# First modulation weights loaded by columns, scale ahead of shift; blocks scaled as they leave PSUM; three first product tiles begun over blocks 0 to 3 while the second half of the shift is still being loaded

## The chip, the cores and the metric

The kernel runs on one NeuronCore of a Trainium2 chip. The metric is the device time of one execution in microseconds (us), as the median of three runs; smaller is better. The engines are TensorE (PE in the rows; PEld is its weight load), VectorE (DVE), ScalarE (ACT), GpSimd (POOL) and SyncE (SP). Each runs its own instructions in order, and they wait for one another by semaphores.

## What is computed

One forward pass of two transformer-like blocks over 512 tokens of width 1024. The first block begins with an adaptive norm, and the change lies there and in the first projection behind it:

```
c_act = silu(c)
mod = (c_act @ w_ada[i] + b_ada[i]).reshape(bsz, 6, D_MODEL)
shift1, scale1 = mod[:, 0], mod[:, 1]          # columns 0..1023 and 1024..2047 of w_ada
u = rms_norm(x, ln1[i]) * (1.0 + scale1) + shift1
proj = u @ w_in                                # then split: ..., z, xbc, dt
dt = softplus(dt + dt_bias)                    # feeds the state space scan, with conv(xbc)
...                                            # scan, projections, FFN; the whole second block
```

## The kernel before

Activations are held by features: a matrix of 1024 x 512 is 8 blocks k of 128 features (partitions) by 512 tokens. Each fp32 product is three products of float32r parts: high x high, high weights x low activations, low weights x high activations. A high part is a rounded copy (ACT, into `whi` or `ahi`), a low part is what is left (DVE, into `wlo` or `alo`). A unit of weights is 1 MB, 1024 x 256, in `raw[0]` or `raw[1]`; it gives two tiles m of 128 features in PSUM banks G, 24 matmuls of 512 columns each (L560 to L562).

At the start `x` (xin, 2 MB) and the shift and scale columns of `w_ada` (eight row blocks `araw`, 1 MB each, 8 KB a partition) are loaded through the DMA queue of ACT (q10). SP's queue (q1) takes 24 vectors, then the 32 columns of `w_in` that give dt (128 B pieces), waits until six of the eight blocks of `w_ada` have landed (`first_landed[5]`), and then loads the first unit of x columns and, unit by unit as buffers come free, all later weights.

DVE multiplies each block of `w_ada` by its part of silu(c) and adds it to `adacc` (L1994 to L1999). TensorE sums `adacc` over the partitions, one column of ones as moving data for each of 16 blocks (L689). DVE makes `coef` = (1 + scale) * ln1 from it (L2028). Meanwhile `x` is turned to features (L652), once for the residual (`xT`) and once after the token factors of the norm (`xs`), and ACT copies the turned `xs` out of PSUM (L1306). Only with `coef` and the shift does ACT make the high parts of the eight blocks (L1320) and DVE the values and low parts (L2035, L1922).

`first_tiles()` on TensorE then goes over the blocks j = 0 to 7: two matmuls of dt (L705, L706, L708) and three of x tile 0 (L711 to L713), each block as soon as its low part is there. x tile 1 follows (`fm_tile`), with `turn_dt` (L724) in its middle: it brings dt back to tokens. Behind it come two tiles of the B and C unit and two of the z unit. TensorE's `keep_clock` matmuls (L646) give no result that is used.

Behind the dt tile hangs a chain in program order: ACT copies it out (L1330) and then splits the B and C unit (L1223), since that unit's high part goes into the buffer that held the dt weights; DVE makes its low part (L1891), the token form of dt (L2057 to L2073), with ACT between (L1343 to L1347), the six convolution steps of the x tiles (L2085), and only then the low part of the z unit (L1891).

## Time and profile before

| | before |
|---|---|
| median of 3 runs | 2228.36 us (2225.49 to 2229.49) |
| the profiled execution's own time | 2229.08 us |
| its span, first to last instruction | 2227.3 us |
| mean granted TensorE clock | 0.992 of full speed |
| TensorE busy in the span | 2194.3 us, 99% |
| first product matmul | 40.12 us after the span's start |
| first matmul of the z unit | 70.41 us |

Times in rows are microseconds from the span's start. A mean of one instruction is in nanoseconds. The granted clock is 1.00 at 2.4 GHz and 0.50 at 1.2 GHz.

### The profile page before, as it was taken

To read this page: it belongs to the slowest core of one execution; us is meant where nothing else is said; L and a number is where in the kernel's file an instruction comes from. 1 tells how busy PE (TensorE), PEld (TensorE's weight loads), DVE (VectorE), ACT (ScalarE), POOL (GpSimd) and SP (SyncE) were. 2 spreads that over 40 slices of the span, in tenths; PEclk is the share of its full clock that TensorE was granted. 3 is DMA by queue.
4 is the path that set the end of the run, shared out by engine and by line. 5 is a ranking of instruction groups with operands and counts; after the bars stand their busy time and mean duration, and the time that the engine had idled before them with its cause. 6 is when DMAs were issued, how large, how long until landed. Compare 5 with 4: busy or idle time off the path is not lost.

```text
span 2227.3 us, 28694 instructions
## 1 busy us (share of the span) xinstructions
PE 2194.3 (99%) x10942; PEld 1833.7 (82%) x10942; DVE 1297.0 (58%) x1831; ACT 858.4 (39%) x1223; POOL 25.2 (1%) x24
## 2 busy tenths in 40 slices
PE   7999999999999999999999999999999999999998
PEld 5888888888888898888888888889878678888887
DVE  5677777767673475434475344354777756434344
ACT  5655555543222342322343222234455444222224
POOL 0000000000000000000000000000001000000000
PEclk8999999999999999999999999999999899999999
DMA  7423323324543334233223322223121002233321
GB/s 254 134 80 106 98 95 104 102 76 157 183 151 103 104 116 132 95 95 97 93 93 101 108 94 95 95 95 93 44 74 39 20 32 83 95 97 99 107 85 67
DMA packets 208141, 222.10 MB, mean 100 GB/s; under 512 B 9413, under 2 KB 200330, under 8 KB 205994
## 3 DMA queue, kind: packets, MB, share of 16 engines
q1 hardware_dynamic: 206362, 210.26, 29.2%
q10 hardware_dynamic: 1680, 10.49, 1.2%
q8 instruction: 66, 1.08, 0.2%
q14 instruction: 33, 0.27, 0.0%
HBM read 218.57 MB, written 2.16 MB: 99 GB/s over the span
## 4 chain that ended last, share of the span: by engine, by line
PE 93%; DVE 3%; DMA 2%; issue 1%; ACT 1%; ACTq 0%; DVEq 0%; SPq 0%
PE G L560 25%; PE G L562 25%; PE G L561 25%; PE G L611 2%; PE G L613 2%; PE G L612 2%; PE G L1065 1%; PE X L778 1%; PE X L1082 1%; DMA araw<-in_w_ada 1%; PE G L574 1%; PE G L576 1%; PE G L575 1%; PE X L1072 1%; PE X L1048 1%
## 5 line engine op out<-in xcount | busy, mean ns | idle before, releaser
L560 PE MATMUL G<-ahi,whi 128*128 128x512 f32 x1472 | 584.6, 397 | 0.0
L562 PE MATMUL G<-ahi,wlo 128*128 128x512 f32 x1472 | 574.5, 390 | 0.0
L561 PE MATMUL G<-alo,whi 128*128 128x512 f32 x1472 | 574.2, 390 | 0.0
L1891 DVE TENSOR_TENSOR wlo<-raw,whi 128x2048 fp32r<-128x2048 f32 (+3 forms) x172 | 386.9, 2249 | 240.8 <-ACT whi L1223 237.8
L1223 ACT ACTIVATE whi<-raw 128x2048 fp32r<-128x2048 f32 (+3 forms) x176 | 330.1, 1876 | 443.0 <-PE G L562 423.5
L560 PEld LDWEIGHTS G<-ahi,whi 128*128 128x128 f32 x1472 | 277.4, 188 | 58.1 <-issue 2.1
L562 PEld LDWEIGHTS G<-ahi,wlo 128*128 128x128 f32 x1472 | 277.0, 188 | 58.4
L561 PEld LDWEIGHTS G<-alo,whi 128*128 128x128 f32 x1472 | 277.3, 188 | 57.8 <-issue 1.9
L560 PE MATMUL G<-hhi,whi 128*128 128x512 f32 x784 | 305.9, 390 | 0.5 <-issue 0.5
L562 PE MATMUL G<-hhi,wlo 128*128 128x512 f32 x784 | 305.1, 389 | 0.0
L561 PE MATMUL G<-hlo,whi 128*128 128x512 f32 x784 | 305.1, 389 | 0.0
L560 PEld LDWEIGHTS G<-hhi,whi 128*128 128x128 f32 x784 | 147.2, 188 | 31.5 <-issue 1.2
L562 PEld LDWEIGHTS G<-hhi,wlo 128*128 128x128 f32 x784 | 147.2, 188 | 30.7
L561 PEld LDWEIGHTS G<-hlo,whi 128*128 128x128 f32 x784 | 147.2, 188 | 30.5 <-issue 0.2
L611 PE MATMUL G<-whi,ahi 128*128 128x256 f32 (+2 forms) x320 | 92.1, 288 | 0.6 <-DVE alo L2474 0.5
L612 PE MATMUL G<-whi,alo 128*128 128x256 f32 (+2 forms) x320 | 90.0, 281 | 0.0
L613 PE MATMUL G<-wlo,ahi 128*128 128x256 f32 (+2 forms) x320 | 89.9, 281 | 0.0
L2085 DVE SCALAR_TENSOR_TENSOR cv<-pre,v1T,cv 128x512 f32<-128x512 f32 x96 | 71.6, 749 | 27.1 <-ACT pre L1355 22.2
L2387 DVE SCALAR_TENSOR_TENSOR xT<-G,xT 128x512 f32<-128x512 f32 x44 | 30.3, 690 | 97.8 <-PE G L562 97.8
L1625 ACT ACTIVATE gs<-gs 128x512 f32<-128x512 f32 x44 | 27.8, 632 | 153.4 <-DVE gs L2542 153.4
L1258 ACT ACTIVATE hhi<-sq 128x512 fp32r<-128x512 f32 x54 | 34.2, 633 | 129.7 <-DVE sq L2551 90.2
L2387 DVE SCALAR_TENSOR_TENSOR xT<-G,modT,xT 128x512 f32<-128x512 f32 x36 | 27.0, 749 | 73.8 <-PE G L562 73.5
(428 smaller groups left out, 2865.8 us busy)
## 6 DMA issues: line engine op xcount, KB each, us to landing
raw<-in_w_in SPq DMA_DIRECT2D x43, 1024.0 KB, 5.1
raw<-in_w_up SPq DMA_DIRECT2D x38, 1024.0 KB, 5.3
raw<-in_w_down SPq DMA_DIRECT2D x32, 1024.0 KB, 5.1
raw<-in_w_gate SPq DMA_DIRECT2D x22, 1024.0 KB, 5.1
braw<-in_w_ada SPq DMA_DIRECT2D x12, 1024.0 KB, 5.2
raw<-in_w_in SPq DMA_DIRECT2D x20, 512.0 KB, 4.4
araw<-in_w_ada ACTq DMA_DIRECT2D x8, 1024.0 KB, 18.0
bc<-acum_dram SPq DMA_DIRECT2D x8, 1024.0 KB, 6.9
```

The lines of the kernel that those rows point to most:

```text
L560: pe.matmul(bank[:], wh[:, j, f], rh[:, j, :], start=(j == 0), stop=False)
L561: pe.matmul(bank[:], wh[:, j, f], rl[:, j, :], start=False, stop=False)
L562: last = pe.matmul(bank[:], wl[:, j, f], rh[:, j, :], start=False, stop=(j == k - 1))
L611: pe.matmul(dst, rh[:, j, tk], wh[:, j, 0:n], start=(j == 0), stop=False)
L612: pe.matmul(dst, rl[:, j, tk], wh[:, j, 0:n], start=False, stop=False)
L613: last = pe.matmul(dst, rh[:, j, tk], wl[:, j, 0:n], start=False, stop=(j == k - 1))
L1223: act.activation(whi[s][:, 0:n], raw[s][:, 0:n], ACT.Copy).then_inc(hi_split, 1)
L1258: act.activation(dst, src, ACT.Copy).then_inc(val_hi, 1)
L1625: act.activation(gs[:, m, :], gs[:, m, :], ACT.Silu).then_inc(sg_ready, 1)
L1891: tt(wlo[s][:, 0:n], raw[s][:, 0:n], r32(whi[s][:, 0:n]), ALU.subtract).then_inc(lo_split, 1)
L2085: ins = stt(cv[:, m, :], pre[:, m, j:j + T], v1T[:, j, bass.ds(blk, 1)], cv[:, m, :], ALU.mult, ALU.add)
L2387: signal(stt(dst, src, gain, dst, ALU.mult, ALU.add), x_ready, "x", g_free[2 * s + m])
```

## The change

The first columns of `w_ada` are loaded in another order and shape: scale first (four pieces of two blocks, 4 KB a row), then the first half of the shift's columns (2 KB a row), then the first unit of x columns (now on ACT's queue too), then the second half of the shift in three pieces. The dt columns move ahead of 21 of the 24 vectors on SP's queue, and SP waits for the last piece of the shift before it loads the next unit.

The scale's first two blocks are multiplied on TensorE alone, the others on DVE, and the sums over partitions now move 128 columns of ones. ACT scales blocks 0 to 3 by `coef` as it takes them out of PSUM and adds the shift in a second operation that makes the high part; then blocks 4 to 7. ACT does all four scalings by the token factors (DVE did two), and loads the table of the square root before `x` has landed. GpSimd takes over the low parts of the dt columns and of the first unit. DVE makes each low part in one operation, and between those of blocks 0 to 3 it adds up the second half of the shift.

`first_tiles()` goes over blocks 0 to 3 with dt and both x tiles (eight matmuls a block), then sums the second half of the shift, turns the vectors, and goes over blocks 4 to 7 with dt and x tile 0, then x tile 1. `turn_dt` is four transposes in place of eight small matmuls, and DVE adds the two halves in one more operation.

```diff
-ahi, alo, xin, *araw = phase(*split_a, ("xin", [P, TB, D]), *((f"araw{u}", [P, UNIT]) for u in range(8)),
-                             ("adacc", [P, UNIT]))
-adacc = araw.pop()
-xn = [araw[k // 4][:, k % 4 * T:(k % 4 + 1) * T] for k in range(KB)]
+ahi, alo, xin, ascale, ashift, adacc = phase(*split_a, ("xin", [P, TB, D]), ("ascale", [P, KB, D]),
+                                             ("ashift", [P, 2, KB, D // 2]), ("adacc", [P, UNIT]))
+xc = [ascale[:, k // 2, k % 2 * T:(k % 2 + 1) * T] for k in range(KB)]
...
-    vec(v2[0:8, :], rows(a["ln1"][0]))
-    vec(v2[8:16, :], rows(a["ln2"][0]))
-    vec(v2[16:64, :], rows(a["b_ada"][0]))
+    sp.dma_start(v2[0:8, :], rows(a["ln1"][0])).then_inc(early_landed, 16)
+    sp.dma_start(v2[8:16, :], rows(a["ln2"][0])).then_inc(early_landed, 16)
+    sp.dma_start(v2[16:64, :], rows(a["b_ada"][0])).then_inc(early_landed, 16)
+    load(w_in[:, :, C_DT:C_DT + HEADS], n=HEADS)
...
-    load(w_in[:, :, C_DT:C_DT + HEADS], n=HEADS)
-    sp.wait_ge(first_landed[5], 16)
-    scan_turn(0, True, False, False)
+    loaded_by_act()
+    sp.wait_ge(first_landed[8], 16)
+    scan_turn(0, True, False, False, True)
...
+    mod = take_x(3)
+    pe.wait_ge(gone, 1)
+    pe.wait_ge(c_ready, 1)
+    pe.wait_ge(first_landed[0], 16)
+    for f in range(KB):
+        for k in range(2):
+            last = pe.matmul(mod[:, f:f + P], ascale[:, k, f * P:(f + 1) * P],
+                             cact[:, k:k + 1].broadcast_to([P, P]), start=(k == 0), stop=(k == 1))
+    last.then_inc(direct_done, 1)
+    pe.wait_ge(early_landed, 16 * EARLY_VECS)
+    pe.transpose(take_x(1)[:, 0:64], v2[0:64, :], ident[0:64, 0:64]).then_inc(aux_done, 1)
+    for k in range(4, KB):
+        turn_features(k, xin).then_inc(tile_done, 1)
     pe.wait_ge(scaled, TB)
-    for k in range(KB):
+    for k in range(4):
         turn_features(k, xs).then_inc(xn_done, 1)
...
+    def sums_by_ones(at, columns, used):
+        t["ada"].add()
+        pe.wait_ge(ada_acc, t["ada"].now())
+        for j, f in enumerate(columns):
+            last = pe.matmul(mod[:, at + j:at + j + P], adacc[:, f * P:(f + 1) * P], ones[:],
+                             start=True, stop=True)
+            if j >= len(columns) - used:
+                last.then_inc(ada_used, 1)
...
+    sums_by_ones(KB, range(KB, KB + 4), 2)
+    sums_by_ones(KB + 4, range(KB + 4, 2 * KB), 2)
+    turn_features(4, xs, take_g(1)).then_inc(xn_done, 1)
+    for k in range(5, KB):
+        turn_features(k, xs, take_x(k - 5)).then_inc(xn_done, 1)
+    sums_by_ones(2 * KB, range(4), 2)
...
-    keep_clock(1, xT[:, 0, :])
-    for f in (*range(KB, 2 * KB), *range(KB)):
-        if f % KB == 0:
-            t["ada"].add()
-            pe.wait_ge(ada_acc, t["ada"].now())
-        last = pe.matmul(X[3][:, f:f + 1], adacc[:, f * P:(f + 1) * P], ones[:, 0:1], start=True, stop=True)
-        if f % KB >= 4:
-            last.then_inc(ada_used, 1)
...
+        banks, wh, wl = [take_g(2 * sx), take_g(2 * sx + 1)], unit(whi[sx]), unit(wlo[sx])
+        keep_clock(FILL_FIRST, banks[0])
...
+        def products(m, j):
+            f = slice(m * P, (m + 1) * P)
+            pe.matmul(banks[m][:], wh[:, j, f], ahi[:, j, :], start=(j == 0), stop=False)
+            pe.matmul(banks[m][:], wh[:, j, f], alo[:, j, :], start=False, stop=False)
+            last = pe.matmul(banks[m][:], wl[:, j, f], ahi[:, j, :], start=False, stop=(j == KB - 1))
+            if j == KB - 1:
+                last.then_inc(tile_done, 1)
+        for j in range(4):
+            if j % 2 == 0:
+                pe.wait_ge(first_low, j // 2 + 1)
+            pe.wait_ge(act_ready, t["op"].now(j + 1))
+            steps(j)
+            for m in range(2):
+                products(m, j)
+        sums_by_ones(2 * KB + 4, range(4, KB), 2)
+        turn_vectors()
+        pe.wait_ge(x_free[2], 1)
+        keep_clock(FILL_SECOND, X[2])
+        pe.wait_ge(lo_split, t["n"].now())
+        for j in range(4, KB):
+            pe.wait_ge(act_ready, t["op"].now(j + 1))
+            steps(j)
+            products(0, j)
+        for j in range(4, KB):
+            if j == 6:
+                turn_dt()
+            products(1, j)
         t["op"].add(KB)
...
-            for half in range(2):
-                last = pe.matmul(bank[:, c * HEADS:(c + 1) * HEADS], ss[0:2 * HEADS, c * P:(c + 1) * P],
-                                 ident[0:2 * HEADS, half * HEADS:(half + 1) * HEADS],
-                                 start=(half == 0), stop=(half == 1))
+            last = pe.transpose(bank[:, 2 * c * HEADS:2 * (c + 1) * HEADS], ss[0:2 * HEADS, c * P:(c + 1) * P],
+                                ident[0:2 * HEADS, 0:2 * HEADS])
         last.then_inc(aux_done, 1)
...
-    for u in range(8):
-        act.dma_start(araw[u][:], a["w_ada"][0][u * P:(u + 1) * P, 0:UNIT]).then_inc(first_landed[u], 16)
+    for u in range(4):
+        ks = slice(2 * u, 2 * u + 2)
+        act.dma_start(ascale[:, ks, :], w_ada[:, ks, D:2 * D]).then_inc(first_landed[u], 16)
+    for u in range(2):
+        ks = slice(4 * u, 4 * u + 4)
+        act.dma_start(ashift[:, 0, ks, :], w_ada[:, ks, 0:D // 2]).then_inc(first_landed[4 + u], 16)
+    act.dma_start(unit(raw[1]), w_in[:, :, C_X:C_X + GW]).then_inc(landed[1], 16)
+    for u, ks in enumerate((slice(0, 4), slice(4, 6), slice(6, 8))):
+        act.dma_start(ashift[:, 1, ks, :], w_ada[:, ks, D // 2:D]).then_inc(first_landed[6 + u], 16)
...
+    act.activation(warm[:], epsT[:], ACT.Sqrt)
...
-    for b in range(2):
+    for b in range(TB):
         act.activation(xs[:, b, :], xin[:, b, :], ACT.Identity, scale=s4[:, b:b + 1]).then_inc(scaled, 1)
...
-    act.wait_ge(xn_free, 1)
-    for k in range(KB):
-        act.wait_ge(xn_done, k + 1)
-        act.activation(xn[k], G[k % 4][:], ACT.Copy).then_inc(g_free[k % 4], 1)
...
+    def scaled_block(k, bank, free):
+        act.wait_ge(xn_done, k + 1)
+        act.activation(xc[k], bank[:], ACT.Identity, scale=coef[:, k:k + 1]).then_inc(free, 1)
+    def shifted(half):
+        act.wait_ge(shift_ready, half + 1)
+        for k in range(4 * half, 4 * half + 4):
+            act.activation(ahi[:, k, :], xc[k], ACT.Identity, bias=modT[:, 0, k:k + 1]).then_inc(val_hi, 1)
+    act.wait_ge(coef_ready, 1)
+    for k in range(4):
+        scaled_block(k, G[k], g_free[k])
...
-    act.wait_ge(coef_ready, 1)
-    for k in range(KB):
-        act.activation(ahi[:, k, :], xn[k], ACT.Identity, scale=coef[:, k:k + 1], bias=modT[:, 0, k:k + 1])\
-            .then_inc(val_hi, 1)
-    t["val"].add(OWN)
-    act.wait_ge(val_hi, KB)
-    for k in range(OWN, KB):
-        act.activation(xn[k], xn[k], ACT.Identity, scale=coef[:, k:k + 1], bias=modT[:, 0, k:k + 1])\
-            .then_inc(own_value, 1)
...
+    shifted(0)
+    scaled_block(4, G[1], g_free[1])
+    for k in range(5, KB):
+        scaled_block(k, X[k - 5], x_free[k - 5])
...
+    shifted(1)
...
+    pool.wait_ge(x_ready, KB)
+    pool.wait_ge(scaled, TB)
+    pool.memset(pacc[:], 0.0).then_inc(gone, 1)
+    pool.wait_ge(hi_split, 1)
+    both = unit(whi[0], KB, 2 * HEADS)
+    pool.tensor_tensor(both[:, :, HEADS:2 * HEADS], unit(raw[0], KB, HEADS), r32(both[:, :, 0:HEADS]),
+                       ALU.subtract).then_inc(lo_split, 1)
+    for c in range(4):
+        if c % 2 == 0:
+            pool.wait_ge(*((hi_split, 2) if c else (first_hi, 1)))
+        cut = slice(c * T, (c + 1) * T)
+        pool.tensor_tensor(wlo[1][:, cut], raw[1][:, cut], r32(whi[1][:, cut]), ALU.subtract)\
+            .then_inc(first_low if c < 3 else lo_split, 1)
     pool.wait_ge(vec_landed, 16 * VECS)
     pool.tensor_copy(v3[0:XB, :].rearrange("b (r d) -> b r d", r=2),
                      dskip[:].unsqueeze(2).broadcast_to([XB, 2, HEAD_DIM])).then_inc(dskip_ready, 1)
-    pool.wait_ge(x_ready, KB)
-    pool.wait_ge(scaled, TB)
-    pool.memset(pacc[:], 0.0).then_inc(gone, 1)
...
-        dve.wait_ge(factor_ready, 1)
-        for b in range(2, TB):
-            ts(xs[:, b, :], xin[:, b, :], s4[:, b:b + 1], None, ALU.mult).then_inc(scaled, 1)
...
+    def weighted(dst, src, k, first=False):
+        c = cact[:, k:k + 1]
+        return ts(dst, src, c, None, ALU.mult) if first else stt(dst, src, c, dst, ALU.mult, ALU.add)
+    scale_acc, shift_acc = adacc[:, D:2 * D], [adacc[:, h * T:(h + 1) * T] for h in range(2)]
     dve.wait_ge(c_ready, 1)
...
+    dve.wait_ge(first_landed[1], 16)
+    for k in (2, 3):
+        link(weighted(scale_acc, ascale[:, k, :], k, k == 2))
+    token_factors()
+    dve.wait_ge(first_landed[2], 16)
+    for k in (4, 5):
+        link(weighted(scale_acc, ascale[:, k, :], k))
+    dve.wait_ge(first_landed[3], 16)
+    link(weighted(scale_acc, ascale[:, 6, :], 6))
+    link(dve.tensor_copy(v2T[:, 0:64], X[1][:, 0:64]))
+    dve.sem_inc(x_free[1], 1)
+    dve.wait_ge(direct_done, 1)
+    link(tt(modT[:, 1, :], X[3][:, 0:KB], badaT[:, KB:2 * KB], ALU.add))
+    for h in range(2):
+        weighted(scale_acc[:, h * T:(h + 1) * T], ascale[:, 7, h * T:(h + 1) * T], 7).then_inc(ada_acc, 1)
+    dve.wait_ge(first_landed[4], 16)
+    for k in range(4):
+        link(weighted(shift_acc[0], ashift[:, 0, k, :], k, k == 0))
+    dve.wait_ge(ada_used, 4)
+    link(tt(modT[:, 1, :], modT[:, 1, :], X[3][:, KB:2 * KB], ALU.add))
+    stt(coef[:], modT[:, 1, :], 1.0, ln1T, ALU.add, ALU.mult).then_inc(coef_ready, 1)
+    dve.wait_ge(first_landed[5], 16)
+    for k in range(4, KB - 1):
+        link(weighted(shift_acc[0], ashift[:, 0, k, :], k))
+    weighted(shift_acc[0], ashift[:, 0, KB - 1, :], KB - 1).then_inc(ada_acc, 1)
+    dve.wait_ge(ada_used, 6)
+    tt(modT[:, 0, 0:4], X[3][:, 2 * KB:2 * KB + 4], badaT[:, 0:4], ALU.add).then_inc(shift_ready, 1)
+    dve.wait_ge(xn_done, KB)
+    for k in range(4):
+        low(alo[:, k, :], ahi[:, k, :], xc[k], modT[:, 0, k:k + 1])
+        if k != 1:
+            dve.wait_ge(first_landed[6 + max(k - 1, 0)], 16)
+        link(weighted(shift_acc[1], ashift[:, 1, 2 * k, :], 2 * k, k == 0))
+        ins = weighted(shift_acc[1], ashift[:, 1, 2 * k + 1, :], 2 * k + 1)
+        if k < 3:
+            link(ins)
+        else:
+            ins.then_inc(ada_acc, 1)
+    dve.wait_ge(ada_used, 8)
+    tt(modT[:, 0, 4:KB], X[3][:, 2 * KB + 4:3 * KB], badaT[:, 4:KB], ALU.add).then_inc(shift_ready, 1)
+    dve.wait_ge(shift_ready, 2)
+    dve.sem_inc(x_free[3], 1)
+    for k in range(4, KB):
+        low(alo[:, k, :], ahi[:, k, :], xc[k], modT[:, 0, k:k + 1])
+    t["ada"].add(8)
+    t["hi"].add(2)
+    aux()
+    dve.tensor_copy(v2T[:, 64:P], X[1][:, P + 64:2 * P])
...
-    def value(k):
-        if k >= 2:
-            dve.wait_ge(act_ready, t["op"].now())
-        signal(ts(sq[:, k % 2, :], xn[k], coef[:, k:k + 1], modT[:, 0, k:k + 1], ALU.mult, ALU.add),
-               val_ready, "val")
-    value(0)
...
-    tt(heads(TMP), X[0][:, 0:P].rearrange("p (c h) -> p c h", c=TB), over(0), ALU.add).then_inc(prep_v, 1)
+    both = X[0][:, 0:2 * P].rearrange("p (c w h) -> p c w h", c=TB, w=2)
+    link(tt(heads(TMP), both[:, :, 0, :], over(0), ALU.add))
+    tt(heads(TMP), both[:, :, 1, :], heads(TMP), ALU.add).then_inc(prep_v, 1)
```

In TensorE's rows the stretch from the turned `xs` to the first block of products looked like this before (L646 `keep_clock`, L668 to L670 the vectors, L689 the sums, L706 on the products of block 0):

```order
L652 MATMUL G<-ident,xs 128x128 x32
L646 MATMUL X<-xT,ones 128x512 x5
L668 MATMUL X<-ident,v 128x128
L669 MATMUL X<-ident,v 128x128
L670 MATMUL X<-ident,v 128x77
L646 MATMUL X<-xT,ones 128x512
L689 MATMUL X<-ones,adacc 128x1 x16
L646 MATMUL X<-xT,ones 128x512
L706 MATMUL G<-ahi,whi 64x512
L708 MATMUL G<-alo,whi 32x512
L711 MATMUL G<-ahi,whi 128x512
```

With the change the same stretch of the same engine is this, up to block 0's first products (L687 sums, L653 `keep_clock`, L735 on the products):

```order
L659 MATMUL G<-ident,xs 128x128 x16
L687 MATMUL X<-ones,adacc 128x128 x8
L659 MATMUL G<-ident,xs 128x128 x4
L659 MATMUL X<-ident,xs 128x128 x12
L687 MATMUL X<-ones,adacc 128x128 x4
L653 MATMUL G<-xT,ones 128x512 x2
L735 MATMUL G<-ahi,whi 64x512
L737 MATMUL G<-alo,whi 32x512
L744 MATMUL G<-ahi,whi 128x512
```

The sums have moved in among the transposes, four of the 16 are gone from here (they come after block 3), the vectors' transposes have gone behind block 3 as well, and two `keep_clock` matmuls stand directly ahead of the products.

On DVE the stretch of the low parts was this before, from the first unit's low part on (L2035 values, L1922 low parts):

```order
L2020 TENSOR_TENSOR wlo<-raw,whi 128x1024
L2022 TENSOR_TENSOR wlo<-raw,whi 128x1024
L2025 TENSOR_TENSOR modT<-X,v2T 128x16
L2028 SCALAR_TENSOR_TENSOR coef<-modT,v2T 128x8
L2035 TENSOR_SCALAR sq<-araw,coef,modT 128x512 x2
L1922 TENSOR_TENSOR alo<-sq,ahi 128x512
L2035 TENSOR_SCALAR sq<-araw,coef,modT 128x512
L1922 TENSOR_TENSOR alo<-sq,ahi 128x512
```

With the change it is this, from the rest of the shift's first half on (L2071 a weighted sum, L2005 a low part):

```order
L2098 SCALAR_TENSOR_TENSOR coef<-modT,v2T 128x8
L2071 SCALAR_TENSOR_TENSOR adacc<-ashift,cact,adacc 128x512 x4
L2104 TENSOR_TENSOR modT<-X,v2T 128x4
L2005 SCALAR_TENSOR_TENSOR alo<-ascale,modT,ahi 128x512
L2071 TENSOR_SCALAR adacc<-ashift,cact 128x512
L2071 SCALAR_TENSOR_TENSOR adacc<-ashift,cact,adacc 128x512
L2005 SCALAR_TENSOR_TENSOR alo<-ascale,modT,ahi 128x512
L2071 SCALAR_TENSOR_TENSOR adacc<-ashift,cact,adacc 128x512 x2
L2005 SCALAR_TENSOR_TENSOR alo<-ascale,modT,ahi 128x512
```

The low parts of the weights are gone from DVE here, and two weighted sums now stand between one low part and the next, four times.

## Rows read from the trace of the kernel before

**Rows 1.** The chain that ended last, 0 to 110 us: start, length, what.

```profile
24.93 9.51 DMA raw<-in_w_in
34.47 1.06 ACT whi L1316
...
40.12 0.66 PE G L706
...
41.20 0.43 PE G L711
```

**Rows 2.** Timeline, 0 to 45 us: start, length, engine, line, operation, tile, count.

```profile
11.92 1.29 DVE L1994 TENSOR_SCALAR adacc<-araw,cact 128x2048 f32<-128x2048 f32 x1 [11.92 <-DMA araw<-in_w_ada]
...
13.77 1.28 ACT L1286 ACT_TABLE_LOAD   x1
...
15.27 2.72 ACT L1292 ACTIVATE xT<-G 128x512 f32<-128x512 f32 x4
...
18.11 2.19 ACT L1300 ACTIVATE xs<-xin,s 128x1024 f32<-128x1024 f32 x2
...
20.96 5.57 PE L652 MATMUL G<-ident,xs 128*128 128x128 f32 x32 [2.22 <-ACTq L1294]
...
31.33 2.48 DVE L1999 SCALAR_TENSOR_TENSOR adacc<-araw,cact,adacc 128x1024 f32<-128x1024 f32 x2 [0.81 <-DMA araw<-in_w_ada]
31.76 0.42 ACT L1311 ACTIVATE whi<-raw 128x256 fp32r<-128x256 f32 x1 [4.49 <-DMA raw<-in_w_in]
```

**Rows 3.** DMA queues, 12 to 27 us: packets, MB, share of 16 engines.

```profile
q10 hardware_dynamic: 802, 5.84, 95.2%
q1 hardware_dynamic: 779, 0.17, 5.6%
```

**Rows 4.** Groups of instructions by form, 0 to 130 us.

```profile
L2085 DVE SCALAR_TENSOR_TENSOR cv<-pre,v1T,cv 128x512 f32<-128x512 f32 x24 | 17.8, 750 | 3.0 <-ACT pre L1355 2.4
L1320 ACT ACTIVATE ahi<-araw,modT,coef 128x512 fp32r<-128x512 f32 x8 | 5.8, 800 | 1.9 <-DVE coef L2028 1.9
L1306 ACT ACTIVATE araw<-G 128x512 f32<-128x512 f32 x8 | 4.2, 600 | 0.2 <-ACT xT L1292 0.2
L757 PE MATMUL X<-xf 128*128 128x128 f32 x8 | 1.1, 275 | 0.0
```

**Rows 5.** GpSimd's groups by form, whole span.

```profile
L1867 POOL TENSOR_TENSOR wlo<-raw,whi 128x512 fp32r<-128x512 f32 x16 | 20.4, 1302 | 1739.5 <-ACT whi L1223 1739.5
L1860 POOL MEMSET pacc<- 128x4096 f32 x1 | 3.5, 3502 | 0.0
```

**Rows 6.** Busy time in stretches; PE, PEld, DVE, ACT, POOL, then the granted clock.

```profile
19.00:21.00 2.00, 0.04 (x1) 0.07 (x2) 1.97 (x1) 1.88 (x4) 0.00 (x0) 1.00 1.02 411
21.00:27.00 6.00, 6.00 (x34) 5.39 (x35) 5.92 (x3) 5.57 (x11) 0.00 (x0) 0.72 1.00 400
...
40.00:52.00 12.00, 11.88 (x41) 8.12 (x42) 6.14 (x11) 6.89 (x10) 0.00 (x0) 0.76 0.20 70
```

**Rows 7.** Timeline behind the dt tile, 51 to 71 us.

```profile
51.44 0.59 ACT L1330 ACTIVATE ss<-G 64x512 f32<-64x512 f32 x1 [5.07 <-PE G L706]
...
54.23 2.29 DVE L1891 TENSOR_TENSOR wlo<-raw,whi 128x2048 fp32r<-128x2048 f32 x1 [7.12 <-ACT whi L1223]
56.85 0.29 DVE L2057 TENSOR_TENSOR dts<-X,dtw 128x128 f32<-128x128 f32 x1 [0.32 <-PE X L724]
59.40 0.23 DVE L2061 TENSOR_SCALAR dts<-dts 128x128 f32<-128x128 f32 x1 [2.26 <-ACT dtw L1345]
...
67.82 2.28 DVE L1891 TENSOR_TENSOR wlo<-raw,whi 128x2048 fp32r<-128x2048 f32 x1
...
70.41 0.39 PE L560 MATMUL G<-ahi,whi 128*128 128x512 f32 x1
```

**Rows 8.** The chain that ended last, from the dt tile on.

```profile
51.17 0.23 PE G L706
...
54.84 1.90 PE X L724 x16
```

More of the change, by code:

```diff
@@ L695, in first_tiles, with steps @@
[L695 removed]
+            def first_tiles(turn_dt):
                 s = next_unit()
                 bank, wd = take_g(2 * s), unit(whi[s], KB, 2 * HEADS)
[L699 to L703 removed]
+                sx = slot[0]
+                slot[0] ^= 1
+                t["n"].add()
+                banks, wh, wl = [take_g(2 * sx), take_g(2 * sx + 1)], unit(whi[sx]), unit(wlo[sx])
+                keep_clock(FILL_FIRST, banks[0])
+                def steps(j):
+                    high, low, dst = wd[:, j, :], wd[:, j, 0:HEADS], bank[0:HEADS, :]
```

119 lines of the change are left out of this document (35 added, 84 removed).

## Prediction

> **What bounds the kernel now.** I read the chain that ended last first: apart from a few microseconds it is TensorE's products, so only a stretch in which TensorE stands still or does something else can give time. The start is such a stretch. There the chain is one transfer after another: the blocks of `w_ada`, then the first unit of x columns, which lands at 24.93 + 9.51 = 34.4 us, then the splits, coef and values, and the first product at 40.12 us [rows 1]. From there the products run without a gap, at first 0.43 us apart at 1.2 GHz, later 0.23 us at 2.4 GHz [rows 1, 8]. The windows say how long: a mean granted clock of 0.76 over 40 to 52 us is (1 - 0.76) / 0.5 x 12 = 5.8 us at the half rate, a loss of 2.9 us against the full one [rows 6].
>
> The second thing to see stands behind the dt tile, whose last matmul starts at 51.17 and ends about 51.4. TensorE has 19.0 us of own work until it starts the z unit at 70.41: 27 products, `turn_dt` (1.90 us), the 48 of B and C. The low part of the z unit is ready at 67.82 + 2.28 = 70.10, by a chain that begins with the end of the dt tile: copy and split on ACT, low part on DVE at 54.23, dt at 56.85 and again at 59.40, convolutions, z's low part [rows 7, 8]. That chain takes 70.10 - 51.4 = 18.7 us, and TensorE comes only 0.3 us after it. Two clocks thus run from the dt tile, nearly equally long, and the change shortens only one of them.
>
> **The change part by part.**
>
> *Transfers.* Seven blocks of `w_ada` landed in 31.33 - 11.92 us, 2.77 us for 1 MB [rows 2]. In the new order the scale's four pieces land at 11.9, 14.7, 17.5 and 20.2, the shift's first half at 23.0 and 25.8, the x unit about 28.7, the rest of the shift by about 34.5. The shorter rows may cost: the x unit (1 KB rows) came 34.44 - 31.33 = 3.1 us behind `w_ada`, 0.35 us more than the 8 KB rows; over the 4 MB of shift at most 1.4 us. I keep 34.5 to 36. The dt columns are 1024 pieces, 64 for each of 16 DMA engines. In 12 to 27 us the two queues moved 802 and 779 packets [rows 3], that is one for one, whatever their size; so those 64 go out beside the 64 packets of 4 KB an engine that make up the scale, and land about 20 us.
>
> The Trainium skill has the same rule (DMA: Bandwidth & Descriptors, Queues, rings and completion order): an engine goes round the rows that have work, but by whole packets of some 9 to 17 descriptors. By that the dt columns would be through in a few turns and land before 12 us. The count of packets in the rows agrees on the turns; nothing later depends on which it is, as ACT only comes to them at 24.5 us.
>
> *ACT and the norm.* The copies of `x` began at 15.27, behind a table load of 1.28 us [rows 2]. Moved ahead of `x`, the load still delays the squares by about 0.6, so I take 0.7 us: copies until 17.3. ACT then does four scalings at 1.10 (two took 2.19) in place of two, until 21.8, and four copies (2.72) until 24.5. TensorE turns blocks 0 to 3 of `xs` as banks come free, until 25.1.
>
> *Scale.* DVE is through with its part about 23.6. TensorE's eight sums follow the transposes: four fp32 matmuls of this form are 8 records in 1.1 us [rows 4], so 2.2 us at 2.4 GHz, about 3.4 at 1.2 GHz. coef is ready at 27.7 or 29.0.
>
> *Shift, first half.* Behind coef DVE still has four weighted sums of 0.75 [rows 4], TensorE four sums, DVE the bias: 32.2 or 34.1. Beside that ACT has four scaled copies (0.6) and the unit's high part in two halves of 1.06 (2.1) [rows 1, 4]. Then 0.8 for the high part of block 0 and 0.8 for its low part: ready at 34.0 to 35.7; I take 34.8. GpSimd needs 1.30 for the piece of low weights that block 0 uses [rows 5], begun about 32, its memset of 3.5 us being over by 28.2: hidden. The two `keep_clock` matmuls ahead take 0.9 each or, at 1.2 GHz, 1.7; only then they reach past the low part, to about 37.
>
> *First half of the products.* Eight matmuls a block are 1.84 us at 0.23, but DVE needs low part and two weighted sums, 3 x 0.75 = 2.25 us, a block. DVE leads: low parts at 34.8, 36.8, 39.0, 41.3, last sum 42.8. This is later than the transfers land, even at 36. Sums 1.1, bias 0.3, ACT 0.7, low part 0.8, semaphores 0.2: block 4 is ready at 45.9. The vectors' transposes and one `keep_clock` lie in this gap. Three blocks of five matmuls (1.15 each) and two more give the end of the dt tile: 45.9 + 3.45 + 0.65 = 50.0 us, against 51.4. A lead of 5.2 us in the first low part has shrunk to 1.4, because blocks 4 to 7 wait for a second round of sum, bias, high and low part. Bounds: 49.2 with 2.4 GHz throughout, 52.1 if `keep_clock` and the first block run at 1.2 GHz.
>
> *Behind the dt tile.* TensorE now has only 15 products left of the x tiles (it did the other 12 before) and a shorter `turn_dt` (0.5): it would reach B and C at 50.0 + 4.0 = 54.0, but their low part needs 5.1 us from the dt tile (54.23 + 2.29 - 51.4), so 55.1. It ends them at 66.0, and z's low part is there at 50.0 + 18.7 = 68.7. The one DVE operation that is added lies where it waited for `turn_dt` (0.32) [rows 7]. z begins at 68.7 in place of 70.41: 1.7 us gained. The products that moved ahead of the dt tile have become waits of 1.1 and 2.7 us.
>
> *The clock.* Waits are not free here. Ahead of 20.96 TensorE waited 2.2 us [rows 2], and the next 6 us had a mean clock of 0.72, which is 3.4 us at 1.2 GHz [rows 6]. Behind z's wait the same would cost 3.4 x 0.5 = 1.7 us. Whether a wait of 2.7 us brings this each time, one execution does not say; I charge half, 0.85.
>
> *Sum.* 2229.08 - 1.7 + 0.85 = 2228.2 for an execution like the profiled one. This lies 0.7 above the median shown, so 2227.5. Everything behind z is the same code with the same waits. Its own range: the dt tile's 49.2 to 52.1 and the clock's 0 to 1.7 give -2.5 to +2.2 us, 2225.0 to 2229.9. Executions differ by about as much (2225.49 to 2229.49). A change under 0.2%, 4.5 us, is what a measurement of this kernel cannot tell from none.
>
> **The rivals.**
>
> *The lead is carried through (faster).* If the first product comes 6 us earlier and neither DVE nor the chain behind dt holds TensorE up, the time is 2228.4 - 6 = about 2222. For it: the transfers bound the start, and they no longer do. Against it: block 4 cannot be ready before a second round of sums, and 18.7 us behind the dt tile is in the rows. It needs a dt tile that ends by 46. Chance 0.15.
>
> *The clock stays at 1.2 GHz (slower).* TensorE waits for banks, for coef and for sums from 18 us on, and before, the clock was at 0.50 for the first 5.8 us of the products although `keep_clock` had run ahead of them [rows 1, 6]. If it stays low through blocks 0 to 3, these take 32 x 0.43 = 13.8 us in place of 9: from 37 to 50.8, block 4 at 53.9, the dt tile at 58, z at 76.7, 6 us late, 2234. It decides once the low stretch reaches past about 43 us. Against it: 32 transposes without a pause ended the low stretch at about 25 us while they ran [rows 2, 6]. Chance 0.07.
>
> The Trainium skill (TensorE: Matmul & The Clock Gate, HAM oscillation) warns of this: a kernel whose bursts are cut by waits is throttled again at each, so work cut in two halves pays twice. The row of 21 to 27 us agrees that a wait is paid for afterwards.
>
> *The dt columns land as late as before (slower).* They used to land about 31.8 us, where ACT splits them (L1311) [rows 2]; if a thousand small packets do so still, ACT stands in front of the scaled blocks until then, coef or not: high part at 32.2, scaled blocks to 34.7, unit to 36.8, block 0's low part at 38.3, 3.5 us later than taken, z 1.8 us later than before, 2231. Rows 3 speak against it. Chance 0.08.
>
> **How the numbers follow.** No measurable change has 0.70 from the first case. The predicted time is its 2227.5. The range reaches from 2222.8, into the faster case, to 2232, over the late dt columns, and leaves out the clock case and half of the faster one. Faster by over 0.2%: most of 0.15 and a tail of the first case, 0.17. Slower: 0.07, part of 0.08 and a tail, 0.12. Within: 0.71.
>
> **What would show it.** In the changed kernel's profile: dt columns split by ACT at 24.5, not later; coef at 27.7 to 29.0; first product at 34 to 37; 2.2 us from one low part to the next on DVE; a gap of TensorE ahead of block 4; the end of the dt tile at 49 to 52; waits ahead of the B and C unit and of z, with DVE's L1972 as releaser; a clock of 0.5 somewhere behind 69 us. The prediction is wrong if z starts before 66 or after 73 us, or if anything behind z has changed its length.

## The result, and the profile after

The changed kernel takes 2250.93 us (median of 5, 2249.21 to 2252.07) against 2228.36 before: a ratio of 1.0102, 95% interval [1.0091, 1.0114]. The median of before is one of 5 executions too, not of 3. The change makes the kernel 22.6 us slower, outside the predicted range. The profiled execution took 2252.07 us, span 2250.3.

The chain of work that ended last in the changed kernel, 0 to 60 us (start, length, what), names the cause in its first rows:

```profile
0.74 0.45 ACTq L1326
1.23 0.52 ACTq L1329
...
3.53 2.07 ACTq L1332
5.63 4.98 ACTq L1332
10.64 5.07 ACTq L1333
15.74 4.22 ACTq L1335
19.99 4.34 ACTq L1335
24.36 1.43 ACTq L1335
25.82 1.28 ACT L1337
27.12 0.19 ACT cact L1337
```

ACTq is ACT's own instruction stream while it hands a transfer to its queue. The rows up to 25.79 compute nothing: a single issuing instruction takes up to 5 us, and ACT does nothing else meanwhile. L1326 loads `x`, L1329 the scale, L1332 and L1335 the halves of the shift, L1333 the x unit. From 3.53 to 25.79 us ACT is held, and its Silu, the squares and all that hangs on them come that much later. The timeline of ACT in the changed kernel (start, length, engine, line, operation, tile, count):

```profile
28.80 1.04 ACT L1344 ACTIVATE sq<-xin 128x1024 f32<-128x1024 f32 x1
...
33.72 2.72 ACT L1351 ACTIVATE xT<-G 128x512 f32<-128x512 f32 x4
36.56 4.27 ACT L1359 ACTIVATE xs<-xin,s 128x1024 f32<-128x1024 f32 x4
```

The copies `xT` began at 15.27 before [rows 2]; they are 18.45 us late here. Coef is made on DVE at 47.19, and the first product starts on TensorE at 54.49 in place of 40.12 [rows 1]. DVE's and TensorE's timeline from there:

```profile
47.19 0.62 DVE L2098 SCALAR_TENSOR_TENSOR coef<-modT,v2T 128x8 f32<-128x8 f32 x1
...
53.19 1.15 DVE L2005 SCALAR_TENSOR_TENSOR alo<-ascale,modT,ahi 128x512 fp32r<-128x512 f32 x1 [0.94 <-ACT ahi L1380]
54.27 1.50 DVE L2071 TENSOR_SCALAR adacc<-ashift,cact 128x512 f32<-128x512 f32 x1
55.81 1.66 DVE L2071 SCALAR_TENSOR_TENSOR adacc<-ashift,cact,adacc 128x512 f32<-128x512 f32 x1
57.50 0.75 DVE L2005 SCALAR_TENSOR_TENSOR alo<-ascale,modT,ahi 128x512 fp32r<-128x512 f32 x1
...
66.77 2.74 DVE L2005 SCALAR_TENSOR_TENSOR alo<-ascale,modT,ahi 128x512 fp32r<-128x512 f32 x4 [0.87 <-ACT ahi L1380]
```

```profile
71.80 0.59 ACT L1401 ACTIVATE ss<-G 64x512 f32<-64x512 f32 x1 [3.23 <-PE G L735]
76.93 0.50 PE L567 MATMUL G<-ahi,whi 128*128 128x512 f32 x1 [1.14 <-DVE wlo L1972]
90.43 0.50 PE L567 MATMUL G<-ahi,whi 128*128 128x512 f32 x1 [2.32 <-DVE wlo L1972]
```

The copy of the dt tile starts at 71.80 (51.44 before [rows 7]), the B and C unit at 76.93, z at 90.43 (70.41 before [rows 7]): 20.0 us late. The span is 2250.3 - 2227.3 = 23.0 us longer. The other 3 us I put down to the clock in the attention part; the windows of before and of the changed kernel, in this order, with the granted clock third from the end of a row:

```profile
1680.00:1820.00 140.00, 134.69 (x772) 103.46 (x770) 100.53 (x294) 67.27 (x182) 20.37 (x16) 0.94 0.10 31
```

```profile
1680.00:1820.00 140.00, 132.94 (x781) 105.99 (x780) 103.84 (x314) 67.20 (x182) 20.38 (x16) 0.91 0.11 34
```

Against 2.4 GHz, 0.94 costs (1 - 0.94) x 140 = 8 us, 0.91 costs 13. The code there is the same, though the two windows lie 20 us apart in it. In the other versions below this stretch cost 5 to 10 us (0.93 to 0.96), whatever they did at the start, so I take it as the scatter of one execution and not as an effect of the change; no run shows this by itself.

**What holds ACT.** Before, the eight issues of `w_ada` took 4.34 us together, and the Silu came at 7.91:

```profile
1.23 4.34 ACTq L1277 DMA_DIRECT2D araw<-in_w_ada  x8
...
7.91 0.18 ACT L1279 ACTIVATE cact<-X 128x8 f32<-128x8 f32 x1 [1.03 <-PE X L640]
```

The page counts what each queue moved in the whole execution. ACT's is q10; first before, then after:

```profile
q10 hardware_dynamic: 1680, 10.49, 1.2%
```

```profile
q10 hardware_dynamic: 4784, 11.54, 1.4%
```

10% more bytes, but 4784 / 16 = 299 pieces for each of the 16 DMA engines in place of 105. A row that lies in one piece in memory is one piece of the transfer: 8 KB each in `w_ada`'s blocks before; 4 KB in the scale, 2 KB in the shift and 1 KB in the x unit now. The queue rows of the changed kernel up to the end of the last issue, 0 to 25.8 us:

```profile
q10 hardware_dynamic: 2771, 8.49, 87.4%
```

So (4784 - 2771) / 16 = 126 pieces for an engine were still waiting when ACT was let go. The same count at the end of the second shift issue (10.6 us) gives 120, of the x unit's (15.7) 153. Before, 1680 pieces less the 297 moved by 5.6 us leave 86, and no issue took over 0.6 us. My theory was now: **an issue ends only when the queue has room for its pieces, some 120 to 155 for each DMA engine.** The rival: the transfers in smaller rows, or the new order of the work, make the start late, and ACT's long rows only show it.

### The profile page after: what moved, and what is told of

It is laid out like the page before. It is cut to its first block, busy times and chain, and to the rows that moved or that the text cites. A ratio compares the mean times of both kernels' runs of the same rounds, so it can differ in the third digit from the quotient of the medians.

```text
span 2250.3 us, 28698 instructions
## 1 busy us (share of the span) xinstructions
PE 2192.2 (97%) x10951; PEld 1834.6 (82%) x10951; DVE 1295.5 (58%) x1840; ACT 858.8 (38%) x1223; POOL 31.4 (1%) x29
## 3 DMA queue, kind: packets, MB, share of 16 engines
q10 hardware_dynamic: 4784, 11.54, 1.4%
## 4 chain that ended last, share of the span: by engine, by line
PE 92%; DVE 4%; ACT 2%; ACTq 1%; issue 1%; DMA 0%; DVEq 0%; SPq 0%
PE G L567 25%; PE G L569 25%; PE G L568 24%; PE G L618 2%; PE G L619 2%; PE G L620 2%; PE G L1116 1%; PE X L829 1%; PE X L1133 1%; PE G L581 1%; PE G L583 1%; PE G L582 1%; PE X L1123 1%; PE X L1099 1%; PE X L837 0%
## 5 line engine op out<-in xcount | busy, mean ns | idle before, releaser
L2169 DVE SCALAR_TENSOR_TENSOR cv<-pre,v1T,cv 128x512 f32<-128x512 f32 x96 | 71.7, 749 | 27.2 <-ACT pre L1426 22.2
L2471 DVE SCALAR_TENSOR_TENSOR xT<-G,xT 128x512 f32<-128x512 f32 x44 | 30.4, 690 | 98.1 <-PE G L569 98.1
```

Of the source, the lines that this page charges most:

```text
L2169: ins = stt(cv[:, m, :], pre[:, m, j:j + T], v1T[:, j, bass.ds(blk, 1)], cv[:, m, :], ALU.mult, ALU.add)
L2471: signal(stt(dst, src, gain, dst, ALU.mult, ALU.add), x_ready, "x", g_free[2 * s + m])
```

## The experiments

Five of the eleven transfers go to SP's queue, in the same order; six with 33 + 4 x 17 + 33 = 134 pieces for each DMA engine stay with ACT. SP hands the five over once the scale's third piece has landed; nothing else changes.

```diff
# SP, behind the vectors
+sp.wait_ge(first_landed[2], 16)
+sp.dma_start(ashift[:, 0, 4:8, :], w_ada[:, 4:8, 0:D // 2]).then_inc(first_landed[5], 16)
+sp.dma_start(unit(raw[1]), w_in[:, :, C_X:C_X + GW]).then_inc(landed[1], 16)
+for u, ks in enumerate((slice(0, 4), slice(4, 6), slice(6, 8))):
+    sp.dma_start(ashift[:, 1, ks, :], w_ada[:, ks, D // 2:D]).then_inc(first_landed[6 + u], 16)
...
```

> The change with its last five early transfers (second piece of the shift's first half, x unit, three pieces of the shift's second half) issued by SP in the same order, once the scale's third piece has landed; ACT keeps x, four scale pieces and one shift piece. Theory 1 (ACT is held while it issues: its queue holds only about 130 outstanding pieces for each DMA engine, and the change gives it about 300): ACT is free at about 5.6 us in place of 25.8, c is there at 8 in place of 27.1, the first product comes at 35 to 38 in place of 54.5, and the time falls by about 20 us, to 2228 to 2232. Theory 2 (the transfers themselves, or the order of the work behind them, make the change late): c is early, but the first product stays behind 48 us and the time above 2243.

Measured: 2230.98 us against 2227.20 of before on the same chip, ratio 1.0016 [1.0007, 1.0025]. Of the 22.6 us above before, 3.8 are left: some 19 are gone. The timeline of this version:

```profile
3.50 2.28 ACTq L1335 DMA_DIRECT2D ashift<-in_w_ada  x1
5.81 1.28 ACT L1337 ACT_TABLE_LOAD   x1 [5.81 <-issue]
...
17.57 4.27 ACT L1359 ACTIVATE xs<-xin,s 128x1024 f32<-128x1024 f32 x4
21.74 2.72 ACT L1351 ACTIVATE xT<-G 128x512 f32<-128x512 f32 x4
24.58 0.42 ACT L1366 ACTIVATE whi<-raw 128x256 fp32r<-128x256 f32 x1
...
36.73 0.42 PE L740 MATMUL G<-ahi,whi 128*64 128x512 f32 x1 [0.32 <-DVE alo L2005]
```

The rival is out: with the same transfers in the same row sizes, and the same order of work, the first product is not late when ACT doesn't issue them. (SP's wait plays no part in this: the last run below leaves it out, in a later version, and nothing comes late.)

The dose between: the second shift piece stays with ACT (167 pieces), four transfers go to SP.

```diff
+act.dma_start(ashift[:, 0, 4:8, :], w_ada[:, 4:8, 0:D // 2]).then_inc(first_landed[5], 16)
```

> As the run before, but the second piece of the shift's first half stays with ACT: only x unit and the shift's second half go by SP. Theory 1: ACT's last issue ends about 10.6 us, 5 us later than in the other version, as the record of the changed kernel shows for that piece; c at 12, squares and copies of x 4 us later; time 0 to 4 us above the other version. Theory 2: no difference between the two.

Measured: 2235.61 us, ratio 1.0036 [1.0023, 1.0050]. That one transfer costs 4.6 us of the median, because its issue takes 5.2 in place of 0.4 on SP:

```profile
3.58 1.94 ACTq L1334 DMA_DIRECT2D ashift<-in_w_ada  x1
5.55 5.18 ACTq L1335 DMA_DIRECT2D ashift<-in_w_ada  x1
```

z starts at 75.80, 4.03 us later than the 71.77 of the version with five.

The other way round: the kernel before, with nothing changed but the size of the pieces. Padding in the SBUF cuts the same 1 MB transfers into rows of 2 KB.

```diff
-*((f"araw{u}", [P, UNIT]) for u in range(8))
+*((f"araw{u}", [P, 4, 512 + 8]) for u in range(8))
...
-act.dma_start(araw[u][:], a["w_ada"][0][u * P:(u + 1) * P, 0:UNIT])
+act.dma_start(araw[u][:, :, 0:512], a["w_ada"][0][u * P:(u + 1) * P, 0:UNIT].rearrange("p (c n) -> p c n", c=4))
...
```

> The kernel before with one thing changed: the eight blocks of w_ada are laid down in the SBUF with 32 bytes of padding behind every 512 numbers, so that the same eight transfers of 1 MB move in pieces of 2 KB in place of 8 KB, in the same order; nothing else differs. 33 pieces an engine for x and 33 for each block: 297 in place of 105. Theory 1: ACT is held until some 25 us, its Silu is at about 26 in place of 7.9, the sums of eight blocks on DVE end about 46 in place of 34, and the time rises by 12 to 16 us, to 2240 to 2245. Theory 2 (the count of pieces does not hold ACT): ACT ends its issues at about 5.6 us as before and the time stays within 3 us of 2228.

Measured: 2236.71 us, ratio 1.0047 [1.0032, 1.0062], where I had 2240 to 2245. The timeline and the queue row of the whole execution:

```profile
1.23 17.25 ACTq L1277 DMA_DIRECT2D araw<-in_w_ada  x8
18.50 1.28 ACT L1279 ACT_TABLE_LOAD   x1 [18.50 <-issue]
```

```profile
q10 hardware_dynamic: 4752, 10.49, 1.3%
```

The bytes and the number of transfers are those of before, the pieces 297 an engine, and the eight issues take 17.25 us in place of 4.3. ACT was free at 18.5, not at my 25: I had carried the changed kernel's end over, which has 1 MB more to move and smaller rows at its end. By 18.5 us q10 had moved 2287 pieces, so (4752 - 2287) / 16 = 154 were left. The first product came at 49.14, 9.0 us late, and the median rose by 9.5. DVE reads the padded rows in the times of before (the last two sums take 2.48 in both) and, once c is there, never waits for a transfer, so neither of these makes it late. This shows the count of pieces as the cause by itself, without any other part of the change.

The same in rows of 4 KB (169 pieces):

```diff
-*((f"araw{u}", [P, UNIT]) for u in range(8))
+*((f"araw{u}", [P, 2, 1024 + 8]) for u in range(8))
...
```

> The kernel before with its eight blocks of w_ada moved in pieces of 4 KB in place of 8 KB (32 bytes of padding behind every 1024 numbers), all else alike: 33 + 8 x 17 = 169 pieces for each DMA engine in ACT's queue. Theory 1 (a limit of about 130 outstanding pieces an engine): the last issues wait until about 40 of them have landed, which is when x has landed: ACT is free at 9 to 10 us in place of 5.6, far before the 18.5 of the version with 2 KB pieces, and Silu is at 11. The sums on DVE started at 11.9 anyway; the time rises by 0 to 4 us. Theory 2 (smaller pieces merely cost more issue time in proportion to their count, 17.25 us for 264): about 9 us for 136, ACT is free at 10 too, but the single issues would be of equal length, 1.1 us each, in place of short ones first and long ones last.

Measured: 2229.25 us, ratio 1.0009 [0.9999, 1.0018]. ACT's issues in this version, two windows of its timeline and its queue row from 0 to 11.3 us:

```profile
1.22 1.04 ACTq L1277 DMA_DIRECT2D araw<-in_w_ada  x2
```

```profile
5.51 2.51 ACTq L1277 DMA_DIRECT2D araw<-in_w_ada  x1
```

```profile
q10 hardware_dynamic: 827, 3.26, 77.0%
```

Half a microsecond each while there is room, then 2.5 to 3 us each, not 1.1 throughout: a piece has no fixed price, a full queue has. (2704 - 827) / 16 = 117 were waiting at the end. ACT was free at 11.3, somewhat later than my 9 to 10, and this hardly costs anything, since the sums of `w_ada` on DVE, which were the chain, began at 11.92 anyway [rows 2].

Then ACT's Silu alone, ahead of the last six transfers of the changed kernel.

```diff
+aux()
+act.activation(cact[:], X[0][:, 0:KB], ACT.Silu).then_inc(c_ready, 1)
 for u in range(2):
     ks = slice(4 * u, 4 * u + 4)
     act.dma_start(ashift[:, 0, ks, :], w_ada[:, ks, 0:D // 2]).then_inc(first_landed[4 + u], 16)
...
-aux()
-act.activation(cact[:], X[0][:, 0:KB], ACT.Silu).then_inc(c_ready, 1)
```

> The change with one instruction moved: ACT's Silu stands ahead of its last six transfers instead of behind all of them. The squares of x still stand behind the issues. Theory 1: c at about 8 us, the scale's weighted sums on DVE are done by 24 us; ACT still issues until about 26 us, the scaled x (xs) comes at 40 as in the change, and the first product at 45 to 48 in place of 54.5; time 2240 to 2245. Theory 2: as the change, 2250, or, if only c counted, 2230.

Measured: 2247.62 us, ratio 1.0089 [1.0074, 1.0105]; c at 7.79, but ACT's last issue still ends at 25.7 and the first product comes at 52.19. It missed the 45 to 48 and the 2240 to 2245. DVE makes two of the scale's sums and then stands 15.6 us in front of the reciprocal of the norm, which needs ACT's squares:

```profile
15.43 1.28 DVE L2071 SCALAR_TENSOR_TENSOR adacc<-ascale,cact,adacc 128x1024 f32<-128x1024 f32 x1
32.35 0.18 DVE L2048 RECIPROCAL s<-s 128x4 f32<-128x4 f32 x1 [15.64 <-ACT s L1345]
...
45.16 0.16 DVE L2097 TENSOR_TENSOR modT<-modT,X 128x8 f32<-128x8 f32 x1 [4.03 <-PE X L687]
```

But this isn't what sets the first product: DVE has all its sums of the scale by 38.4, goes on to the shift's, and then waits 4.03 us for TensorE's, which stand behind the turned `xs`. `xs` is made until 39.3 here and until 40.8 in the changed kernel, and from there it is 13 to 14 us to the first product in either (turning, sums, coef, the first half of the shift). My 45 to 48 left too little for these. An early c is worth 2 to 3 us while the squares stand behind the issues.

**What was left of the prediction's error.** The version with five by SP ends 3.8 us above before, where I had 0.9 below. Its DVE shows one place, its GpSimd the other side of it:

```profile
35.84 0.75 DVE L2005 SCALAR_TENSOR_TENSOR alo<-ascale,modT,ahi 128x512 fp32r<-128x512 f32 x1 [0.94 <-ACT ahi L1380]
36.51 1.52 DVE L2071 TENSOR_SCALAR adacc<-ashift,cact 128x512 f32<-128x512 f32 x1
38.06 0.75 DVE L2071 SCALAR_TENSOR_TENSOR adacc<-ashift,cact,adacc 128x512 f32<-128x512 f32 x1
```

```profile
34.76 1.27 POOL L1937 TENSOR_TENSOR wlo<-raw,whi 128x512 fp32r<-128x512 f32 x1
35.99 1.76 POOL L1937 TENSOR_TENSOR wlo<-raw,whi 128x512 fp32r<-128x512 f32 x1
```

GpSimd's last part starts during DVE's low part and takes 0.5 us longer than the one before; DVE's TENSOR_SCALAR, 0.49 elsewhere, ends at 38.03, 0.3 behind the end of that part at 37.75. In the changed kernel the three DVE rows shown above lose 1.15 - 0.75, 1.50 - 0.49 and 1.66 - 0.75, 2.3 us in all. The test gives DVE the low part, in two halves, in the time in which it waited for sums; GpSimd's four parts go:

```diff
+dve.wait_ge(first_hi, 1)
+tt(wlo[1][:, 0:half], raw[1][:, 0:half], r32(whi[1][:, 0:half]), ALU.subtract).then_inc(first_low, 1)
+dve.wait_ge(hi_split, 2)
+dve.wait_ge(lo_split, 1)
+tt(wlo[1][:, half:UNIT], raw[1][:, half:UNIT], r32(whi[1][:, half:UNIT]), ALU.subtract).then_inc(lo_split, 1)
 dve.wait_ge(ada_used, 6)
...
```

> The version with five transfers by SP, and the low part of the first x unit made by DVE in two halves of 1.15 us (while it waits for the shift's sums, 31.8 to 34.7 us) in place of four parts on GpSimd. Theory A (GpSimd's work on the SBUF holds DVE up, 1.5 us in place of 0.5 for the TENSOR_SCALAR behind the first low part): that one takes 0.5 again, the step from the first low part to the second is 2.2 us in place of 3.0, everything behind it 0.8 earlier, time 0.5 to 1 us less. Theory B (it was long for another reason, as its first use or the DMA's writing): the duration stays at 1.5 and the time unchanged or up.

Measured: 2229.45 us, ratio 1.0008 [0.9999, 1.0017].

```profile
36.50 0.75 DVE L1999 SCALAR_TENSOR_TENSOR alo<-ascale,modT,ahi 128x512 fp32r<-128x512 f32 x1 [0.94 <-ACT ahi L1380]
37.17 0.48 DVE L2065 TENSOR_SCALAR adacc<-ashift,cact 128x512 f32<-128x512 f32 x1
```

The operation takes 0.48 with the same operands and the same transfers running; the next low part follows after 1.97 us in place of 3.01. So GpSimd's work beside it was the reason. The gain does not go through, though: the first low part itself starts 0.66 us later, since DVE's second half of the weights' low part stands ahead of the bias, and z starts at 71.41, 0.36 us earlier and not 0.8. The intervals of the two versions overlap; the medians, 1.5 us apart, show a direction at most.

The Trainium skill (SBUF — State Buffer, Who interferes with whom) has such interference as a lock: GpSimd uses DVE's second pair of ports, and whoever comes first holds it for the whole instruction. The rows fit a lock: GpSimd's 1.27 and DVE's 0.49 both grow while the other is at work, and DVE's ends just behind GpSimd's. They don't prove one: DVE's low part at 35.84 begins 0.19 us before the end of GpSimd's third part (34.76 + 1.27) and takes its usual 0.75, and spans on GpSimd are rough.

Next, which of the two clocks behind the dt tile counts. For blocks 4 to 7, the dt tile's eight matmuls go first:

```diff
 for j in range(4, KB):
     pe.wait_ge(act_ready, t["op"].now(j + 1))
     steps(j)
+for j in range(4, KB):
     products(0, j)
```

> The version with five transfers by SP, and for blocks 4 to 7 the dt tile's eight matmuls run ahead of the x tiles' 24. Theory A (the chain of 18.7 us behind the dt tile sets the start of z, TensorE's own work does not): the dt tile ends at 51.4 in place of 53.6, no wait ahead of B and C, z starts at 70.0 to 70.3 in place of 71.8, time 1.5 to 2 us less. Theory B (TensorE's own work sets it): z starts at 71.8 as before.

Measured: 2227.07 us, ratio 0.9999 [0.9989, 1.0008]. In this execution block 4's low part starts at 47.25, 0.9 us earlier than in the version without the edit (48.12), because its bias came 2.3 us earlier, with the clock up (below). The dt copy is at 50.73, 3.5 us behind it in place of 5.0, and z at 69.36, 18.6 behind the copy: 1.5 us of the 2.4 are the edit's. The wait ahead of B and C is gone, that ahead of z is 1.70. The chain behind the dt tile sets z.

All together, and TensorE's sums at two places ahead of transposes that nobody waits for:

```diff
-for k in range(4):
+for k in range(2):
     turn_features(k, xs).then_inc(xn_done, 1)
 sums_by_ones(KB, range(KB, KB + 4), 2)
 sums_by_ones(KB + 4, range(KB + 4, 2 * KB), 2)
-turn_features(4, xs, take_g(1)).then_inc(xn_done, 1)
+for k in range(2, 4):
+    turn_features(k, xs).then_inc(xn_done, 1)
 for k in range(5, KB):
     turn_features(k, xs, take_x(k - 5)).then_inc(xn_done, 1)
+turn_features(4, xs, take_g(1)).then_inc(xn_done, 1)
 sums_by_ones(2 * KB, range(4), 2)
...
```

> Five transfers by SP, the low part of the first unit by DVE, dt tile first, and TensorE's order changed at two places: the scale's sums ahead of turning blocks 2 and 3 of the scaled x, and block 4 turned after blocks 5 to 7 so that the sums of the shift's first half do not wait for ACT's scaled block 1. Each should bring what it removes from the chain: coef at 27.2 (28.6), bias of the first half at 32.5 (34.7), first low part at 33.6 (35.8), dt tile's end at 48 (53.6), z at 67 (71.8); time 2226 to 2227, level with or 1 us under the kernel before. If TensorE's own work sets z, it comes at 69 and the time is 2228.

Measured: 2225.86 us against 2227.35, ratio 0.9990 [0.9981, 0.9999]: the one version whose interval lies under 1, if barely. Coef is at 27.28 and z at 68.25 (I had 67). What each of the two orders of TensorE is worth was not run by itself, and coef moves with the clock too: 28.61 and 27.66 in two versions with the same code up to there. The bias of the first half came at 33.81, not 32.5, which the next run looks at: the second half of DVE's low part stood ahead of it.

```diff
-dve.wait_ge(hi_split, 2)
-dve.wait_ge(lo_split, 1)
-tt(wlo[1][:, half:UNIT], raw[1][:, half:UNIT], r32(whi[1][:, half:UNIT]), ALU.subtract).then_inc(lo_split, 1)
 dve.wait_ge(ada_used, 6)
```

(The three lines stand ahead of the wait for the second half's sums instead.)

> The version with all four edits, and the second half of the unit's low part on DVE (1.22 us), which only blocks 4 to 7 need, moved from ahead of the first half's bias to behind the shift's last weighted sum, where DVE waits for TensorE's sums. Theory A (DVE's order sets the bias: it stood behind the low part at 33.81 us although TensorE's sums were through at about 32.6): bias at 32.7, first low part at 33.8 in place of 34.9, dt tile and z 1.1 us earlier, z at 67.1, time 0.5 to 1.1 us less, 2225. Theory B (something else ends the wait there, as the x unit that landed at 30.4 or ACT): no change.

Measured: 2226.64 us, ratio 0.9992 [0.9983, 1.0001]. Bias at 32.74, first low part at 33.84, z at 67.20, 1.05 us earlier, all as theory A says; the time shows nothing of it. A microsecond is less than one low stretch of the clock in the attention part, which comes or doesn't.

Last, the order between the queues, by leaving out SP's wait:

```diff
-sp.wait_ge(first_landed[2], 16)
```

> The version with all four edits without SP's wait for the scale's third piece ahead of the five transfers that it issues. Theory A (the queues take turns piece by piece, and the dt columns' 64 pieces an engine stand ahead in SP's queue, so the five get their turn only when the scale is through): scale's last piece still lands at 20 to 21, time the same within 1 us. Theory B (what is issued early takes bandwidth from what is needed first): the scale comes 1 to 3 us later, the first product and the time with it.

Measured: 2225.82 us, ratio 0.9997 [0.9988, 1.0006]. DVE gets the scale's last piece at 20.18 (20.63 with the wait). Handing the five over early takes nothing from the scale. z was at 68.90 in this execution, 0.65 later than with the wait: TensorE came early, waited 1.92 us for the first low part, and had a mean granted clock of 0.66 over 35 to 40 us, during the first products; its sums for blocks 4 to 7 were late by that. With the wait, the low stretch fell on the sums and the `keep_clock` matmuls instead (the latter took 3.04 us in place of 1.88), and only 0.38 us of waiting was left.

## Why the prediction was wrong

**The step that failed** is the start of *ACT and the norm*: copies of `x` from 15.27, "behind a table load", moved by 0.7 us. It takes ACT's times from before, as if handing over eleven transfers cost what handing over nine did. The transfers were counted as bytes on the DMA engines and, for the dt columns, as pieces that take turns; ACT's own issues of them had no term at all. They took until 25.82, where the 105 pieces of before let ACT go in time for its Silu at 7.9. Pieces in place of bytes was the right unit; I used it for one queue of the two and for landing times alone. No rival covered it either: all three began behind an ACT that is on time.

The other steps can be read in the version with five transfers by SP, in which that step holds:

| step | predicted | five by SP | changed kernel |
|---|---|---|---|
| scale's last piece on DVE | 20.2 | 20.41 | waits for c |
| copies, scalings, copies done on ACT | 17.3, 21.8, 24.5 | 17.4, 21.8, 24.5 | 36.4, 40.8, 43.5 |
| dt columns split | 24.5 | 24.58 | 43.58 |
| coef | 27.7 to 29.0 | 28.8 | 47.8 |
| low part of block 0 ready | 34.8 | 36.6 | 54.3 |
| first product | 34 to 37 | 36.73 | 54.49 |
| low part of block 4 ready | 45.9 | 48.9 | 67.5 |
| dt tile's end | 50.0 | 53.1 | 71.7 |
| z | 68.7 | 71.77 | 90.43 |

- *Transfers, dt columns, norm*: right to 0.3 us once ACT is free. The x unit came at 30.4 (where ACT had to wait for it, in the last versions) in place of 28.7.
- *First low part*, 1.8 us late: mostly the clock of this execution. The version with the dt tile first has the same code up to there, and its first low part is ready at 33.55 + 1.26 = 34.8, as predicted. TensorE turns blocks 4 to 7 ahead of the first half's sums and waits for ACT's scaled block in both; behind that wait the mean clock was 0.50 over 31 to 34 us in the one, and 1.00 over 30 to 33 in the other. The bias was at 34.73 and 32.45, where the prediction has 34.1 at 1.2 GHz and 32.2 at 2.4. TensorE's rows with five by SP, then with the dt tile first:

```profile
30.18 0.78 PE L664 MATMUL G<-ident,xs 128*128 128x128 f32 x4 [1.87 <-ACT ascale L1374]
30.75 2.77 PE L664 MATMUL X<-ident,xs 128*128 128x128 f32 x12
33.31 1.39 PE L692 MATMUL X<-ones,adacc 128*128 128x128 f32 x8
```

```profile
29.18 0.66 PE L664 MATMUL G<-ident,xs 128*128 128x128 f32 x4 [1.82 <-ACT ascale L1375]
29.68 1.47 PE L664 MATMUL X<-ident,xs 128*128 128x128 f32 x12
31.26 1.16 PE L692 MATMUL X<-ones,adacc 128*128 128x128 f32 x8
```

- *2.25 us a block*: 2.24 measured, except the first block: 3.01, in the changed kernel 4.31, without GpSimd beside it 1.97. It is the longer, the more of GpSimd's four parts are still to come when the low part starts: 4.42 with the dt tile first. There block 4 is ready at 48.0, so the early bias gained less than 1 of its 2.3 us. GpSimd's low part was "hidden" from TensorE but not from DVE.
- *Behind the dt tile*: 18.7 us was right in every version (18.6, from the copy: 71.80 to 90.43, 53.15 to 71.77, 50.73 to 69.36), and so were the waits: 1.14 for 1.1 and 2.3 for 2.7.
- *Clock*: behind z's wait of 2.3 us a low stretch followed in three versions (those with five and four by SP, and with the low part on DVE) and not in the changed kernel nor with Silu first; behind 1.7 us in none. So half is no worse a charge than the runs allow, and an execution pays all or nothing. The rival with the clock at 1.2 GHz did not happen: in the changed kernel the clock was low over 42 to 46 us (mean 0.62), ahead of the first product, and at 2.4 GHz through the products behind it.
- *The rivals*: "the lead is carried through" needed a dt tile by 46; 48.5 is the earliest that any version had. The dt columns were never late: issued at 2.69 in the version with five, they took 17.0 us to land, about 20 as the count had it; the other time given for them, before 12, did not come. Part of the first products did once run at 1.2 GHz, in the version without SP's wait, at a price of 0.65 us for z.

With the failed step mended and these two terms as that execution had them (1.8 up to the first low part, 1.2 from block 0 to block 4), z is at 68.7 + 1.8 + 1.2 = 71.7, as measured. The time needs more care. The prediction lay 0.9 us under before; 3.0 more for z and the other half of the low stretch behind it, 0.85, make it 3.0 above, and 3.8 was measured on the same chip (2230.98 against 2227.20). The last 0.8 is not explained. The remaining 19 us of the 22.6 are ACT's issues, which end at 25.8 in place of 5.6.
